# Four edits to a one-core transformer layer: gathers, sums of squares, feature order, memory queries

## The reference, cut to what matters

```
h += W_out [ GLA (4 heads) || stick-breaking (8 heads) ](RMSNorm(h))
h += MemCrossAttn(RMSNorm(h), RMSNorm(mem))      # 4 heads, 256 memory tokens
h += PEER(RMSNorm(h))                            # 128^2 experts, 8 heads, top 16
out = RMSNorm(h)                                 # 1024 tokens x 1024 features, f32

# GLA: chunks of 64 tokens, a state carried from chunk to chunk
o = (q*exp(b)) @ state + tril(q.k with decay) @ v
state = state*exp(b_last) + (k*exp(b_last-b)).T @ v
# PEER: per token and head, scores against 2 x 128 keys, top 16 of the sums, then
out[t] += sum_k gate_k * gelu(u[e_k] . x[t]) * v_emb[e_k]
```

## Time and profile before

| | |
|---|---|
| profiled execution | 3705.7 us, span of its instructions 3703.9 us |
| runs | 3705.04, 3706.51, 3707.81 us |
| busy in the span | PE 2896.9, DVE 2554.9, ACT 1501.5, POOL 1518.9 us |
| linear attention | 152.7 to 304.5 us |
| mixout, memnorms | to 671.8 us, 672.1 to 700 us |
| memory attention | 796.9 to 847.4 us |
| ffnnorm, key scores | 894.3 to 915.6 us, to 1021.4 us |
| experts | 1021.7 us to the end |

### The profile page before, as it was taken

One profiled execution on the slowest core, in us unless ns is written; L12 is line 12 of the kernel. 1 busy time (PEld: TensorE's weight loads), 2 busy tenths in 40 slices (PEclk: granted clock), 3 DMA queues, 4 the chain that ended last, 5 costly groups with the idle time before them and its releaser, 6 DMA issues.

```text
span 3703.9 us, 32338 instructions
## 1 busy us (share of the span) xinstructions
PE 2896.9 (78%) x8696; PEld 1456.9 (39%) x8696; DVE 2554.9 (69%) x5661; ACT 1501.5 (41%) x3958; POOL 1518.9 (41%) x1176
## 2 busy tenths in 40 slices
PE   6999999787978788777877888776766666766666
PEld 5777544676823233333333333322222222222222
DVE  3453454534467887888778877877787788778776
ACT  3221596322233534554344433344343434434342
POOL 0000111000055544555445545555556655556654
PEclk8999999898989899989999999888889888888988
DMA  2101002212299999999999999999999999999998
GB/s 80 41 23 46 1 1 103 84 65 68 69 392 418 418 414 417 405 411 419 411 415 409 416 409 416 403 410 416 413 410 420 413 408 420 413 417 413 413 418 345
DMA packets 177612, 1155.95 MB, mean 312 GB/s; under 512 B 19984, under 2 KB 22048, under 8 KB 46240
## 3 DMA queue, kind: packets, MB, share of 16 engines
q0 software_dynamic: 147456, 1073.81, 70.5%
q1 hardware_dynamic: 29984, 80.26, 6.2%
HBM read 1149.80 MB, written 4.19 MB: 312 GB/s over the span
## 4 chain that ended last, share of the span: by engine, by line
DMA 39%; PE 11%; ACT 8%; issue 7%; DVE 5%; POOL 2%; POOLq 0%; DVEq 0%; ACTq 0%
DMA expert_rows<-in_uv,choice_index 39%; PE expert_acc L2166 11%; DVE expert_rows L1940 2%; ACT L2042 2%; POOL expert_rows L1774 2%; ACT L1360 2%; DVE expert_own_acc L1914 1%; ACT expert_wt L2044 1%; ACT expert_dg L2053 1%; ACT expert_wt L2042 1%; ACT choice_best L1360 1%; PE expert_side L2092 0%; ACT L1991 0%; DVE expert_dot L1940 0%; ACT expert_spare L1991 0%
## 5 line engine op out<-in xcount | busy, mean ns | idle before, releaser
L2166 PE MATMUL expert_acc<-expert_rows,expert_dg 128*128 128x512 f32 x3072 | 1689.8, 689 | 670.6 <-ACT expert_dg L2053 667.4
L1774 POOL DMA_INDIRECT expert_rows<-in_uv,choice_index x1024 | 1469.3, 1435 | 1295.1 <-PE expert_acc L2166 737.5
L1940 DVE CUSTOM_DVE_ANT_0 expert_rows<-expert_rows,expert_xn 128x1024 f32<-128x1024 f32 x1024 | 1251.9, 1223 | 560.7 <-DMA expert_rows<-in_uv,choice_index 554.8
L2166 PEld LDWEIGHTS expert_acc<-expert_rows,expert_dg 128*128 128x128 f32 x3072 | 615.5, 215 | 1685.5 <-ACT expert_dg L2053 1116.7
L2042 ACT ACTIVATE expert_wt<-expert_dot 128x1 f32<-128x1 f32 x1024 | 207.5, 203 | 1486.6 <-DVE expert_dot L1940 1485.7
L1914 DVE SCALAR_TENSOR_TENSOR expert_own_acc<-expert_rows,expert_wt,expert_own_acc 128x1024 f32<-128x1024 f32 x248 | 317.7, 1281 | 3.5 <-ACT expert_wt L2044 3.5
L2053 ACT ACTIVATE expert_dg<-ident,expert_wt 128x128 f32<-128x128 f32 x768 | 308.4, 402 | 25.2
L2044 ACT ACTIVATE expert_wt<-expert_wt,choice_gate 128x1 f32<-128x1 f32 x1024 | 301.4, 294 | 33.4
L2077 PE MATMUL expert_side<-expert_w_raw,mix_b 128*128 128x512 f32 x256 | 128.7, 605 | 0.0
L1060 POOL TENSOR_SCALAR_AFFINE_SELECT heads<-heads 128x128 f32<-128x128 f32 x64 | 20.7, 323 | 262.8 <-DVE heads L1124 262.6
L2092 PE MATMUL expert_side<-z_b,expert_w_raw 128*128 128x512 f32 x256 | 126.2, 595 | 0.0
(11 more groups left out here) (356 smaller groups left out, 3684.4 us busy)
## 6 DMA issues: line engine op xcount, KB each, us to landing
expert_rows<-in_uv,choice_index POOLq DMA_INDIRECT x1024, 12.2
H<-in_x SPq DMA_DIRECT2D x8, 1024.0 KB, 10.2
pq_w_raw<-in_w_pq SPq DMA_DIRECT2D x16, 512.0 KB, 3.6
expert_w_raw<-in_w_pq SPq DMA_DIRECT2D x32, 256.0 KB, 8.9
stick_w_raw<-in_w_feat SPq DMA_DIRECT2D x8, 512.0 KB, 3.6
tok_w_raw<-in_w_tok SPq DMA_DIRECT2D x8, 512.0 KB, 3.8
out_w_raw<-in_w_out SPq DMA_DIRECT2D x8, 512.0 KB, 6.4
mk_w_raw<-in_w_mk SPq DMA_DIRECT2D x8, 512.0 KB, 3.6
```

The costliest lines, as they stand in the source:

```text
L1774: pool.indirect_dma_start(out=rows[R % ROWS], out_offset=None, in_=uv, in_offset=bass.IndirectOffsetOnAxis(ap=index[:, q, r:r + 1], axis=0 ...
L1940: nc.vector.tensor_tensor_reduce(rows[R % ROWS][:, 0:D], rows[R % ROWS][:, 0:D], xn[:, :], 1.0, 0.0, ALU.mult, ALU.add, dot[:, h % 2, r:r ...
L2166: last_mm = nc.tensor.matmul(acc[:, h * HALF:(h + 1) * HALF], dg[:, n % DG, :], rows[R % ROWS][:, D + h * HALF:D + (h + 1) * HALF], start= ...
```

## The change

**Gathers.** A class `Ring` holds the 7 rows; 4 of them are allocated ahead of the key scores, whose POOL list now waits for the first group's index and issues the first 4 gathers. The expert phase skips these. The gain vector `gf` is loaded at the end of the key scores' SP list, and the experts' first step no longer waits for the final gain vector `gl` (which is waited for in `finish`).

**Sums of squares.** `mixout` and `memout` get `squares`: behind its weight splits ACT squares and sums each block as soon as DVE has added its last bank (the 2 memory blocks earlier), and `norm_phase` leaves its own sums out.

**Features.** `half(0, 0, 0)` is issued before the blocks; in block b PE makes `half(b, s, 1)` behind the transposes and `half(b+1, 1-s, 0)` between the chunks. DVE empties h=0 at the start of `attend(b)`, and h=1 before the chunks. PE's loop is written out.

**Memory queries.** PE reads the queries in `q_t` directly; `mem_qb` and its copies go, and PE waits for the exponentials of the block two before.

```
 norm_phase(..., sums=None)
+        ms = sums or co.sb(f"{name}_ms", [P, nb], ctx=cx)
-            for b in range(0, nb, 2):
+            for b in range(0, 0 if sums else nb, 2):          # ACT; DVE alike
 token_gemm_phase, ACT, behind the weight splits
+            if squares:
+                link = Chain(act, squared)
+                for b in range(first, nb + before):
+                    if b < before:
+                        act.wait_ge(extra, 16 * len(loads))
+                    else:
+                        act.wait_ge(bank_free, nb * n_chunks + b - before + 1)
+                    link(nc.scalar.activation(junk[:, :], tok(b), ACT.Square, accum_out=ms[:, b:b + 1]))
 gla_phase, DVE attend(b, s)
                 link.restart()
+                empty(b, 0)
                 dve.wait_ge(scores, b + 1)
...
                 dve.sem_inc(masked, 1)
-                empty(b, 0)
+                empty(b, 1)
                 for c in range(NC):
-                    if c:
-                        empty(b, 1)
                     dve.wait_ge(sums, 2 * b + c + 1)
 gla_phase, PE
-            with pe.Fori(0, NB // 2) as i:
-                for s in range(2):
-                    b = 2 * i + s
+            half(0, 0, 0)
+            for b in range(NB):
+                s = b % 2
...
                     last.then_inc(turned, 1)
-                    half(b, s, 0)
+                    half(b, s, 1)
...
                 for c in range(NC):
-                        if c:
-                            half(b, s, 1)
+                    if c and b + 1 < NB:
+                        half(b + 1, 1 - s, 0)
                     wait_alone(co, pe, state_ready, 2 * b + c + 1)
 memory_attention_phase
-            def queries(b, s):
-                act.wait_ge(s_full, b + 1)
-                nc.scalar.activation(qb[:, s, :, :], q_t[:, :, ds(b * P, P)], ACT.Copy).then_inc(q_ready, 1)
...
-                pe.wait_ge(q_ready, b + 1)
+                if b >= 2:
+                    pe.wait_ge(probs, MEM_HEADS * (b - 1))
-                   nc.tensor.matmul(ps[s][:, h, :], qb[:, s, HD * h + k, :], k_t[:, HD * h + k, :], ...
+                   nc.tensor.matmul(ps[s][:, h, :], q_t[:, HD * h + k, b * P:(b + 1) * P], k_t[:, HD * h + k, :], ...
 key_scores_phase
+            pool.wait_ge(index_ready, 1)
+            for R in range(ring.EARLY):                          # EARLY = 4, ROWS = 7
+                ring.gather(pool, R, choice.index[:, 0, R:R + 1], uv)
...
+            sp.dma_start(gf[:, :], g_ffn.broadcast_to([P, D])).then_inc(gain_landed, 16)
+            sp.wait_ge(gain_landed, 16)
 expert_phase
-            sp.dma_start(gf[:, :], g_ffn.broadcast_to([P, D])).then_inc(gains_landed, 16)
+                    if R < ring.EARLY:
+                        continue
...
-                else:
-                    dve.wait_ge(gains_landed, 32)
 program
+            token_gemm_phase(co, "mixout", ..., squares=(tok_q, sums_q, 0, MB))
+            token_gemm_phase(co, "memout", ..., squares=(lambda b: co.H[:, b, :], sums_f, 0, 0))
```

More of the change, by code:

```diff
@@ L181, in rstd_steps, with norm_phase @@
         link(nc.vector.tensor_tensor(y, y, t, ALU.mult))
-def norm_phase(co, name, tok, nb, gain, place, rstd, loads=()):
+def norm_phase(co, name, tok, nb, gain, place, rstd, loads=(), sums=None):
     nc = co.nc
@@ L248, in _ @@
             link = Chain(dve, done)
-            for b in range(1, nb, 2):
+            for b in range(1, 0 if sums else nb, 2):
                 if loads:
@@ L433, in token_gemm_phase @@
         banks = [cx.enter_context(nc.psum_tensor(f"{name}_bank{j}", [P, HALF], F32)) for j in range(nb)]
+        if squares:
+            tok, ms, first, before = squares
+            squared = co.sem(f"{name}_squared")
+            junk = cx.enter_context(nc.psum_tensor(f"{name}_junk", [P, D], F32))
         block = cx.enter_context(nc.Block())
@@ L824, in _ @@
                         for a in range(2):
[L825 to L835, removed]
-                    half(b, s, 0)
-                    pe.wait_ge(masked, b + 1)
-                    pe.wait_ge(values, b + 1)
-                    pe.wait_ge(o_free, 2 * b + 2)
+                            last = nc.tensor.matmul(po[h][rows, a, :], qi[feats, s, a, rows], state[feats, c, a, :],
+                                                    start=False, stop=(c == NC - 1), skip_group_check=True)
@@ L868, in gla_phase @@
+                            hd = 2 * a + h
+                            last = nc.tensor.matmul(pst[c][feats, a, :], kt[rows, s, hd * GLA_DK:(hd + 1) * GLA_DK],
+                                                    vb[rows, s, hd * GLA_DV:(hd + 1) * GLA_DV], start=True, stop=True)
+                    last.then_inc(sums, 1)
     co.end_phase()
@@ L1239, in body @@
                 if more:
-                    queries(b + 2, s)
                     exps(b + 2, s)
-            for b in range(2):
-                queries(b, b)
             for b in range(2):
@@ L1437, in select, with __init__, complete, gather @@
         yield
-def key_scores_phase(co, act_t, w, sub_keys, scores, choice):
+class Ring:
+    ROWS = 7
+    EARLY = 4
+    def __init__(self, co, ctx):
+        self.co = co
+        self.landed = [co.nc.alloc_semaphore(name=f"row_landed{j}") for j in range(self.ROWS)]
+        early = co.sb("early_rows", [P, self.EARLY, 2 * D], ctx=ctx, side="right")
+        self.rows = [early[:, j, :] for j in range(self.EARLY)]
+    def complete(self, ctx):
+        self.co.phase_sems += self.landed
+        late = self.co.sb("rows", [P, self.ROWS - self.EARLY, 2 * D], ctx=ctx)
+        self.rows += [late[:, j, :] for j in range(self.ROWS - self.EARLY)]
+    def gather(self, pool, R, index, uv):
+        pool.indirect_dma_start(
+            out=self.rows[R % self.ROWS], out_offset=None, in_=uv,
+            in_offset=bass.IndirectOffsetOnAxis(ap=index, axis=0),
+            bounds_check=NKEYS * NKEYS - 1, oob_is_err=False).then_inc(self.landed[R % self.ROWS], 16)
+def key_scores_phase(co, act_t, w, sub_keys, scores, choice, ring, uv, gf, g_ffn):
     nc = co.nc
@@ L1669, in expert_phase @@
         sb = lambda n, shape, dt=F32: co.sb(f"expert_{n}", shape, dt, ctx=cx)
-        ring = sb("rows", [P, ROWS, E])
-        rows = [ring[:, j, :] for j in range(ROWS)]
-        gf, gl = sb("gffn", [P, D]), sb("gfinal", [P, D])
+        ring.complete(cx)
+        rows = ring.rows
+        gl = sb("gfinal", [P, D])
         xn, hb = sb("xn", [P, D]), sb("hb", [P, D])
```

99 lines of the change are left out of this document (55 added, 44 removed).

## The result

The changed kernel takes 3724.41 us, the median of 5 runs (3722.61 to 3725.53), against 3706.51: a ratio of 1.0046, interval 1.0035 to 1.0058. It is slower, by 17.9 us. Its profiled execution took 3725.5 us, with a span of 3723.8.

The account below looks back on a forecast made before the run. The last stage was taken as bound by DMA gathers, linear attention by DVE and PE chains of nearly one length. +40.0 - 9.7 - 3.2 - 11 = +16.1 us gave a median of 3722.5, range 3708 to 3733.

Parts of the forecast that it names:

- linear attention: Linear attention: PE's h=1 half waits for DVE's bank copy behind the next block's operands; +40.0 us including the clock.
- of it the clock: Linear attention: after PE's wait each half starts at the low clock, 2.0 us more for seven blocks, +14.0.
- memory queries: Memory attention: reading queries in place removes PE's waits for ACT's copies and a lost clock; -9.7 us.
- squares: Norms: squares moved into the projections bring the logarithm forward, 2.2 us in `memnorms` and 1.0 in `ffnnorm`; -3.2.
- first gathers and gain: Last stage: four rows gathered early and the gain loaded early let its stream start four rows further on; -11 us.
- rival in which PE's order sets the period: Linear attention: the h=0 copy comes before operand work or is not waited for, PE works through; 3664 us, chance 0.07.
- The clock holds: Linear attention: PE's clock does not fall in the gap, so the stage costs no 14.0; 3708.6 us, chance 0.14.
- The four pieces: Memory attention: first query copy 1.1 us, block 2's wait 4.1, its lost clock 2.5, block 3's wait 2.0, all saved.
- 10.7 less, and a little for the 0.5 MB of gain: Last stage: the fifth row's dot product takes the first's place, 10.7 us sooner, plus a little from the gain's absence.
- worst case of +3: Key scores: early gathers share the DMA engines with weight loads, so weights come late; at most +3 us, 0 taken.

Follow-up runs that it names:

- gap filled: Changed kernel with 20 unread 128 x 512 matmuls before the h=1 half of blocks 0 to 6, state-sum banks sharing one: 3710.9 us.
- the two banks: Changed kernel with one feature bank for each half, the two state-sum banks put into one, order of PE and DVE unchanged: 3680.83 us.

## Why the prediction was right

3722.5 was forecast and 3724.4 measured, within the range, and by the forecast mechanism. That the sum came within 2 us is partly luck: taken out alone, the squares measured 1.7 us less than forecast and the memory queries 1.5 more, which nearly cancel.

| term | forecast | trace of the changed kernel | part taken out alone |
|---|---|---|---|
| linear attention | +40.0 | +39.9 | 39.9 |
| of it the clock | +14.0 | +13.8 | 13.9 (gap filled) |
| memory queries | -9.7 | -9.9 | 11.2 |
| squares | -3.2 | -2.2 and -1.1 at the logarithms, the 1.1 given back | 1.5 |
| first gathers and gain | -11 | -11.2 at the 16th dot product, -13.0 at the end | rows 8.5, gain 5.9, not additive |

**Linear attention.** The trace value is the way from DVE's first instruction of the stage (152.67 before, 154.61 after) to the next stage's first product (311.69 before, 353.52 after), 39.9 us longer. The new period was put together as 22.87 at full clock; with the gap filled it is 22.97. Its first piece, 7.50 from the state update to the end of the operands, is 7.48, and the copy, the half and the 6.83 behind the second half's start follow as summed. The rest is the clock: 2.0 a block was taken from the first block of before, whose row gives 2.2 (7.88 less 5.59 and 0.1). The seven halves behind a wait take 7.06, 8.42, 7.61, 7.14, 8.44, 7.61 and 7.16 us (218.93 to 226.54 is the third) against 5.67 at full clock, so 1.4 to 2.8 each and 13.8 in all. The last block gave its half back.

The order of DVE's list decided it. The copy that PE needs is one instruction of 0.7 us, and DVE had nothing else against it than that it stands behind 7.5 us of work for the next block. The rival in which PE's order sets the period fell for this kernel, but it is the case of the two banks: there PE needs no copy and the time is 3680.8, and 3668.5 once the masks are ahead as well. The prediction's figure for it, 3664, also supposed that PE never waits for DVE. The Trainium skill ("Perfetto Trace Analysis", section "Matmuls") asks for independent groups of products to rotate through different PSUM banks, so that the evacuation of one overlaps the products of the next. The two kernels with and without the second bank agree with it, at 44.0 us apart.

**The clock holds** was the rival with the best chance beside the forecast, and the filled gap shows both that it fell and what it would have been: 3710.9, where 3708.6 was worked out. The Trainium skill ("TensorE: Matmul & The Clock Gate", section "HAM oscillation — how this bites in real kernels"), whose rule on bursts parted by waits stood beside the 14.0, is borne out: behind each of the seven waits for the copy, of 4.59 to 6.13 us, the half starts at 0.50.

**Memory queries.** The four pieces came nearly as they were read. From the first scores to `memout` the stage took 50.14 us before (798.04 to 848.18) and takes 41.05, and the wait ahead of the first scores fell from 2.29 to 1.50: together 9.9 less.

**Squares.** 2.2 and 1.1 at the logarithms against 2.2 and 1.0. The term was still too large: it took for granted that an earlier logarithm moves everything behind it. In `ffnnorm` the 1.0 was given back before the last stage began. Taken out alone the part measured 1.5 where 3.2 was forecast, with spreads of 2 to 3 us.

**First gathers.** The step "10.7 less, and a little for the 0.5 MB of gain" holds at the start of the stage: the 16th dot product is 11.2 us nearer to the first DMA, of which the runs give 9.3 to the four rows (10.1 would be four megabytes at 414 GB/s) and 1.9 to the gain, for which the first step no longer waits, nor for the other. The lead is 10.7 at the 144th dot product. The 13.0 at the end of the span lies at the far end of what the traces of either code allow (9.3 to 13.2). The gathers were issued at 1020.90, and not as soon as the index was written (1016.34): the signal that POOL waits for comes later in DVE's list. They kept the DMA engines busy until about 1037, so they were done some 17 us before the last stage and not 25. That was overlooked, and it cost nothing.

**Weights beside the gathers.** The worst case of +3 did not come. DMA issues from 1005 to 1056 (count, KB each, median us from issue to landing), first in the changed kernel, then in the one without early gathers:

```profile
pq_w_raw<-in_w_pq SPq DMA_DIRECT2D x4, 512.0 KB, 5.7
...
gffn<-in_g_ffn SPq DMA_DIRECT2D x1, 512.0 KB, 8.8
```
```profile
pq_w_raw<-in_w_pq SPq DMA_DIRECT2D x4, 512.0 KB, 3.3
...
gffn<-in_g_ffn SPq DMA_DIRECT2D x1, 512.0 KB, 4.5
```

The transfers do get in each other's way: the weights land 2.4 us later and the gain 4.3. But each weight is asked for a tile ahead, and ACT's splits in the key scores still wait for PE alone. The longer landings lie in slack: from the logarithm of `ffnnorm` to the last stage it is 123.34 us in the run without `squares`, which has the early gathers, and 123.35 before.

**What the sum doesn't hold.** The four trace values with the squares at 3.3 give 39.9 - 9.9 - 3.3 - 13.0 = +13.7, and the span grew by 19.9. 1.9 of the rest arose before linear attention starts. Of the other 4.3, some 1.2 stand between the logarithm of `ffnnorm` and the last stage, where every kernel with the squares moved is 0.7 to 1.2 longer. Another 1.3 stand between `memout`'s first product and that logarithm, where the changed kernel's profile has 50.42 us and the nine others with this code 49.04 to 49.33. The last 1.7 stand between the first product behind linear attention and the logarithm of `memnorms`, a stretch that takes 362.3 to 365.0 us with the same code. Why these stretches move was not traced.

## What to carry to other kernels

When work is moved ahead on one engine, look up where the instruction that frees its buffer stands in the other engine's list: a copy of 0.7 us behind 7.5 us of the next block's work set the period here, and a second bank was worth 44 us. Price an idle TensorE twice, once for the gap and once for the low clock behind it, and where something frees the engine's next step, put it ahead of work that only a later block needs. Data brought in early is only worth its bytes when everything else that its first use needs is there too. And follow a saving past its own stage, to a fixed point behind it: the 1.1 us of `ffnnorm` were gone there.

## What the runs showed of the hardware

- The price of a fallen clock was not constant: after waits of 6.12 and 6.13 us the half took 1.5 us more in one block and 2.8 in another, according to where in it the full clock came back (in the window from 199 for a half begun at 193.22, in the one from 223 for one begun at 218.93, in the one from 247 for one begun at 243.82).
- Work that starts earlier can meet a lower clock: 8 transposes of `ffnnorm` took 1.10 us at 1.00 where the norm made its own sums, and 16 took 3.64 at 0.50 where it began 1.1 us earlier.
- 1.56 us without a product between the filling products and the half left the granted clock at 1.00; in the gap of 6.12 us it was at 0.52 in the window from 189, with PE idle since 187.1.
- Four gathers of 1 MB among the weight loads raised the landing of a 512 KB piece (median of four) from 3.3 to 5.7 us and that of the gain from 4.5 to 8.8.
- Taking the load of a 512 KB gain, and the wait for both gains, out of the stage's start was worth 1.9 us with late rows and 5.0 with early ones (16th dot product).
